# Gated recurrence: score blocks of four tokens as one product around a middle reference, five levels above instead of seven

## The reference

```python
qf = silu(q) * DK ** -0.5
z  = clip(f, -30, 30)
logf = minimum(log_sigmoid(z) + log1p(lb * exp(-z)), 0)      # g, one per token and channel
kf = -expm1(logf)                                            # 1 - decay
# inside a chunk, bcum = cumsum(g):
attn[i, j] = sum_d qf[i, d] * exp(bcum[i, d] - bcum[j, d]) * kf[j, d]     for j <= i
o = attn @ v + (qf * exp(bcum)) @ state
state = exp(b_last) * state + (kf * exp(b_last - bcum)).T @ v
```

## Time and profile before

| | us |
|---|---|
| median of 3 runs | 2405.66 (2405.41 to 2405.76) |
| span of the profiled execution | 2404.5 |
| TensorE busy | 2388.6 (99%) |
| VectorE busy | 1676.1 (70%) |
| GpSimd busy | 1253.3 (52%) |
| ScalarE busy | 811.7 (34%) |
| the heads, from the first head's diagonal to the last head's keys | about 619.6 to 1049.2 |

### The profile page before, as it was taken

One profiled execution on the slowest core, in us unless ns is written; L12 is line 12 of the kernel. 1 busy time (PEld: TensorE's weight loads), 2 busy tenths in 40 slices (PEclk: granted clock), 3 DMA queues, 4 the chain that ended last, 5 costly groups with the idle time before them and its releaser, 6 DMA issues.

```text
span 2404.5 us, 31465 instructions
## 1 busy us (share of the span) xinstructions
PE 2388.6 (99%) x11815; PEld 1967.3 (82%) x11815; DVE 1676.1 (70%) x1837; ACT 811.7 (34%) x1187; POOL 1253.3 (52%) x936
## 2 busy tenths in 40 slices
PE   9999999999999999999999999999999999999998
PEld 6888888888888888888888888888887888888887
DVE  7889888888878888878865637652896534444464
ACT  4443442554222222221122214253444434342422
POOL 0677773343022332223767766745667656666564
PEclk9999999999999999999999999999999999999999
DMA  7322323111211111124854445522532212121243
GB/s 284 140 80 105 127 110 123 62 61 61 78 44 44 44 44 44 44 97 144 277 199 149 140 140 167 181 91 71 177 129 75 92 62 97 59 99 57 84 175 123
DMA packets 93193, 263.28 MB, mean 109 GB/s; under 512 B 8736, under 2 KB 14112, under 8 KB 92064
## 3 DMA queue, kind: packets, MB, share of 16 engines
q1 hardware_dynamic: 77536, 227.26, 27.3%
q10 hardware_dynamic: 15552, 34.61, 4.1%
...
## 4 chain that ended last, share of the span: by engine, by line
PE 94%; DVE 3%; issue 1%; ACT 1%; DMA 0%; SPq 0%; POOL 0%; ACTq 0%; DVEq 0%
PE ps L537 25%; PE ps L538 25%; PE ps L539 25%; PE xb L537 2%; PE xb L538 2%; PE xb L539 2%; PE xa L537 2%; PE xa L539 2%; PE xa L538 2%; PE ps L630 1%; PE xb L771 1%; PE xb L800 1%; PE xb L803 1%; PE xa L791 1%; DVE mt_lo L1138 0%
## 5 line engine op out<-in xcount | busy, mean ns | idle before, releaser
L2822 POOL TENSOR_TENSOR small<-small 128x1 f32<-128x1 f32 x172 | 53.6, 311 | 794.8 <-PE ps L539 620.9
L2825 POOL TENSOR_TENSOR w_lo<-w_raw,w_hi 128x1024 fp32r<-128x1024 f32 x172 | 444.5, 2584 | 14.4
L537 PE MATMUL ps<-h_hi,w_hi 128*128 128x512 f32 x928 | 368.0, 397 | 0.0
L539 PE MATMUL ps<-h_hi,w_lo 128*128 128x512 f32 x928 | 362.0, 390 | 0.0
L538 PE MATMUL ps<-h_lo,w_hi 128*128 128x512 f32 x928 | 361.7, 390 | 0.0
L2911 POOL TENSOR_TENSOR m_lo<-m_raw,m_hi 128x512 fp32r<-128x512 f32 x144 | 200.3, 1405 | 146.1 <-ACT m_hi L2203 142.8
L537 PE MATMUL ps<-yb_hi,w_hi 128*128 128x512 f32 x608 | 238.7, 393 | 0.0
L539 PE MATMUL ps<-yb_hi,w_lo 128*128 128x512 f32 x608 | 236.6, 389 | 0.0
L538 PE MATMUL ps<-yb_lo,w_hi 128*128 128x512 f32 x608 | 236.6, 389 | 0.0
L537 PEld LDWEIGHTS ps<-h_hi,w_hi 128*128 128x128 f32 x928 | 174.3, 188 | 36.9 <-issue 0.2
L539 PEld LDWEIGHTS ps<-h_hi,w_lo 128*128 128x128 f32 x928 | 174.2, 188 | 37.0
...
## 6 DMA issues: line engine op xcount, KB each, us to landing
...
```

The costliest lines, as they stand in the source:

```text
L537: nc.tensor.matmul(out, wh, xh, start=start, stop=False, skip_group_check=onto)
L539: return nc.tensor.matmul(out, wl, xh, start=False, stop=stop, skip_group_check=onto)
L2822: nc.gpsimd.tensor_tensor(small[:, 13:14], small[:, 12:13], small[:, 12:13], ALU.add)
L2825: nc.gpsimd.tensor_tensor(w_lo[:, u], w_raw[:, u], w_hi[:, u].bitcast(F32), ALU.subtract).then_inc(w_split, 1)
```

## The change

The bottom two levels and the diagonal go; blocks of four tokens are scored directly, as one product. In a block of four the reference time is in the middle: the earliest token's key is multiplied by a decay, its query by the inverse of one, the middle token's key and query are copied, and the two latest tokens' queries are multiplied by decays and their keys by inverses. The inverses 1/f are made as the square of Abs_reciprocal_sqrt on ScalarE (`decay_inverses`: three ACTIVATE of 256 elements, a Square and a Copy with scale -1, each of 768), corrected on VectorE by one Newton step (`base_keys`). The decays are kept above 9e-14 (`LEAST`). The products of these keys and queries (`base_blocks`, again 16) replace the diagonal, and their scores enter `attn` through a mask (`base_out`). Five levels, of blocks of 4 to 64, follow. `kr`, `qpf`, `vt` and `zc` serve as scratch, so ScalarE's copy of `vt` now waits until the base keys and queries are ready (`lv_ready`). TensorE runs the whole of tile `i` before `base_blocks`, then waits for tile `g` at once. Levels 1 and 2 stand where levels 3 and 4 stood, 3 and 4 where 5 and 6 stood, 5 where 7 stood.

```diff
@@ -33,7 +33,8 @@
 KEPT = KB // 2
 CHUNK = 128
 NCH = T // CHUNK
-LEVELS = 7
+BASE = 4
+LEVELS = 5
 TIME_ORDER = (0, 1, 2, 3, 7, 6, 5, 4)
 CW, LW = 31, 4
 FFB = 4
@@ -41,6 +42,7 @@
 KV_RING = 6
 EPS = 1e-6
 CLIP = 30.0
+LEAST = 9e-14
 LRU_C = 8.0
 DK_SCALE = float(P) ** -0.5
 XA_HEADS = 4
...
@@ -511,6 +513,7 @@
         down_loaded = [*kvw_loaded, *s_loaded[1], lg_loaded]
         DOWN_OLD = [first + 32 for first in KV_FIRST[:4]] + [16 * (SEVENS // 2)] * 2 + [16 * KB // 2]
         y_gained, GAINED_OLD = mem_rt, 1
+        inv_ready, inv_done, INV_OLD = lm_ready, lmult_done, KB
         HEAD_PAIR = N_HG // 2 + 1 - M0 - SEVENS
         SUM_OLD, BLOCK_OLD, PART_OLD, UP_OLD = 4 * SEVENS, 7 * SEVENS, 3 * SEVENS, 16 * (SEVENS - SEVENS // 2)
@@ -522,6 +525,12 @@
 
             x = x[:]
             return bass.AP(x.tensor, x.offset + at0, [x.ap[0], [step, 2], [skip, n], [one, c]])
+
+        INV = HALF + HALF // 2
+
+        def inv_early(x):
+
+            return pairs(x, HALF, HALF // BASE, HALF // BASE, 1, 1)
 
         def turned(x, n):
@@ -754,7 +763,7 @@
 
             def level(h, l):
 
-                pe.wait_ge(lv_ready, LEVELS * h + l)
+                pe.wait_ge(lv_ready, (LEVELS + 1) * h + l + 1)
                 pe.wait_ge(lv_free, (LEVELS + 1) * h + max(l - 1, 1))
                 w = CHUNK // 2
                 bank = xb[:, (l % 2) * HALF:(l % 2 + 1) * HALF]
@@ -771,11 +780,11 @@
                         mm = nc.tensor.matmul(out_, keys, queries, start=True, stop=True, tile_position=(0, side * w))
                 mm.then_inc(lv_done, 1)
 
-            def diagonal_blocks(c, ch):
+            def base_blocks(c, ch):
                 w = CHUNK // 2
                 for side in range(2):
                     cols = slice(c * CHUNK + side * w, c * CHUNK + (side + 1) * w)
-                    mm = nc.tensor.matmul(xb[side * w:(side + 1) * w, cols], hg["k"][:, cols], hg["q"][:, cols],
+                    mm = nc.tensor.matmul(xb[side * w:(side + 1) * w, cols], hg["kr"][:, cols], hg["qpf"][:, cols],
                                           start=True, stop=True, tile_position=(0, side * w))
                 return mm
@@ -839,26 +848,17 @@
                     full_tile(m, 1)
                 else:
                     tiles_beside_tail(m, h)
-                take(m + 1, 0)
-                half_of(0, 0)
-                if first(h):
-                    quarter_of(0, 1, 0)
-                pe.wait_ge(evac[1], m + 1)
+                full_tile(m + 1, 0)
+                pe.wait_ge(lv_ready, (LEVELS + 1) * h + 1)
                 if not first(h):
                     pe.wait_ge(oc_done, h)
-                per_chunk(NCH, diagonal_blocks).then_inc(diag_done, 1)
-                if first(h):
-                    quarter_of(0, 1, 1).then_inc(mm_done, 1)
-                else:
-                    half_of(0, 1).then_inc(mm_done, 1)
-                level(h, 1)
-                level(h, 2)
+                per_chunk(NCH, base_blocks).then_inc(base_done, 1)
                 take(m + 1, 1)
                 quarter_of(1, 0, 0)
                 quarter_of(1, 0, 1)
                 quarter_of(1, 1, 0)
-                level(h, 3)
-                level(h, 4)
+                level(h, 1)
+                level(h, 2)
                 quarter_of(1, 1, 1).then_inc(mm_done, 1)
                 pe.wait_ge(evac[0], m + 2)
                 if not first(h):
@@ -1518,32 +1518,78 @@
 
             zc, sp_, sn, f, b, k, q, gg = (hg[x] for x in ("zc", "sp", "sn", "f", "b", "k", "q", "gg"))
 
+            def earliest(x):
+
+                return pairs(x, 0, HALF + BASE - 1, HALF // BASE, BASE, 1)
+
+            def middle(x):
+
+                return pairs(x, 1, HALF + 1, HALF // BASE, BASE, 1)
+
+            def latest(x):
+
+                return right(x, BASE // 2)
+
             def queries(h, l, last):
 
-                c = 2 ** (l - 1)
+                c = BASE * 2 ** (l - 1)
                 s.wait(last)
-                if l > 1:
-                    mul(merged(hkp[l % 3], c), left(k, c), left(b, c))
+                mul(merged(hkp[l % 3], c), left(k, c), left(b, c))
                 mul(packed(hqp[l % 4], c), right(q, c), right(f, c)).then_inc(lv_ready, 1)
 
+            def spread(c):
+
+                done(mul(left(b, c), left(b, c), right_end(f, c)))
+                return s.at(mul(right(f, c), right(f, c), left_end(f, c)))
+
             def widen(h, l):
 
-                c = 2 ** (l - 1)
-                dve.wait_ge(lv_ready, LEVELS * h + l)
-                if l == 1:
-                    done(v.tensor_copy(left(b, c), right(f, c)))
-                else:
-                    done(mul(left(b, c), left(b, c), right_end(f, c)))
-                return s.at(mul(right(f, c), right(f, c), left_end(f, c)))
+                dve.wait_ge(lv_ready, (LEVELS + 1) * h + l + 1)
+                return spread(BASE * 2 ** (l - 1))
+
+            def first_decays(h, last):
+
+                s.wait(last)
+                done(v.tensor_copy(left(b, 1), right(f, 1)))
+                mul(right(f, 1), right(f, 1), left_end(f, 1)).then_inc(inv_ready, 1)
+
+            def base_keys(h):
+
+                dve.wait_ge(inv_ready, INV_OLD + h + 1)
+                dve.wait_ge(inv_done, INV_OLD + h + 1)
+                inv, first_, minus = zc[:, 0:INV], hg["qpf"], hg["vt"]
+                mul(packed(zc, 2), latest(f), packed(first_, 2))
+                done(mul(inv_early(zc), earliest(b), inv_early(first_)))
+                done(v.scalar_tensor_tensor(minus[:, 0:INV], inv, -2.0, minus[:, 0:INV], ALU.add, ALU.mult))
+                mul(earliest(hg["kr"]), earliest(k), earliest(b))
+                v.tensor_copy(middle(hg["kr"]), middle(k))
+                mul(latest(hg["kr"]), latest(k), packed(minus, 2))
+
+            def base_queries(h):
+
+                mul(earliest(hg["qpf"]), earliest(q), inv_early(hg["vt"]))
+                v.tensor_copy(middle(hg["qpf"]), middle(q))
+                mul(latest(hg["qpf"]), latest(q), latest(f)).then_inc(lv_ready, 1)
+
+            def base_out(h):
+
+                dve.wait_ge(base_done, h + 1)
+                w = CHUNK // 2
+                v.memset(small[:, 14:15], 0.0)
+                for side in range(2):
+                    part = slice(side * w, (side + 1) * w)
+                    out_, scores = (x[part, :].rearrange("p (n c) -> p n c", c=CHUNK)[:, :, part] for x in (hg["attn"], xb))
+                    ins = v.copy_predicated(out_, lvmask[part, 0].rearrange("p (n c) -> p n c", c=w), scores)
+                ins.then_inc(lv_free, 1)
 
             def scores_out(h, l):
 
-                c = 2 ** (l - 1)
+                c = BASE * 2 ** (l - 1)
                 dve.wait_ge(lv_done, LEVELS * h + l)
                 dve.wait_ge(lv_free, (LEVELS + 1) * h + l)
                 v.memset(small[:, 14:15], 0.0)
                 bank = xb[:, (l % 2) * HALF:(l % 2 + 1) * HALF]
-                v.copy_predicated(right(hg["attn"], c), packed(lvmask[:, l - 1], c), packed(bank, c)).then_inc(lv_free, 1)
+                v.copy_predicated(right(hg["attn"], c), packed(lvmask[:, l], c), packed(bank, c)).then_inc(lv_free, 1)
 
             def states(h):
@@ -1602,49 +1648,41 @@
                     cleared = s.at(v.memset(hg["attn"][:], 0.0))
                 dve.wait_ge(hsig, 2 * h + 2)
                 done(v.scalar_tensor_tensor(f[:], sn[:], lb, sp_[:], ALU.mult, ALU.add))
-                s.at(v.tensor_scalar(f[:], f[:], 1.0, None, ALU.min))
+                s.at(v.tensor_scalar(f[:], f[:], 1.0, LEAST, ALU.min, ALU.max))
                 s.at(v.tensor_scalar(k[:], sn[:], lb1, 0.0, ALU.mult, ALU.max))
-                s.at(v.tensor_scalar(merged(hkp[1], 1), left(sn, 1), lb1, 0.0, ALU.mult, ALU.max))
-                last = s.at(v.memset(right(b, 1), 1.0))
+                first_decays(h, s.at(v.memset(right(b, 1), 1.0)))
                 if not first(h):
                     squares_low(h)
                     gated = gated_output(h, m)
+                base_keys(h)
                 dve.wait_ge(hsigq, h + 1)
                 for n in range(2):
                     ins = v.scalar_tensor_tensor(q[:, n * HALF:(n + 1) * HALF], turned(ps[1], n), DK_SCALE, turned(hg["qs"], n),
                                                  ALU.mult, ALU.mult)
                 ins.then_inc(evac[1], 1)
                 dve.wait_ge(evac[1], m + 1)
-                queries(h, 1, last)
-                last = widen(h, 1)
-                dve.wait_ge(ylru_stored, 16 * KB // 2)
-                queries(h, 2, last)
+                base_queries(h)
                 if not first(h):
                     normed_output(h, gated)
-
-                dve.wait_ge(diag_done, h + 1)
+                dve.wait_ge(ylru_stored, 16 * KB // 2)
+                dve.wait_ge(lv_ready, (LEVELS + 1) * h + 1)
+                queries(h, 1, spread(BASE // 2))
                 if first(h):
                     s.wait(cleared)
```

(40 more changed lines are left out.)

8 lines of the change are left out of this document (4 added, 4 removed).

## The result

| | before | after |
|---|---|---|
| median, us | 2405.70 (2405.41 to 2405.76, 4 runs) | 2422.22 (2421.75 to 2422.26, 4 runs) |
| ratio to before | | 1.0068, 95% interval 1.0054 to 1.0083 |
| span of the profiled execution | 2404.5 | 2420.4 |

The change makes the kernel 16.5 us slower. The forecast was 2408.4 with a range up to 2416: wrong in size, and outside the range. The profiled execution took 2422.19, so what lies around the span is 1.8 us. The forecast had 1.2 for it, from a span and a median of different executions.

A forecast was written before the change was run, and what follows sets the result against it. TensorE, busy 99%, bounds the kernel, with VectorE close behind at kr. Head 0 +5.3 and heads 1 to 6 -2.6 give +2.7 on the span of 2404.5, 2407.2; plus 1.2 to the median: 2408.4 us, range 2401 to 2416 (own range 2404 to 2413).

The forecast's parts named there:

- TensorE's saving: Each head on TensorE: one group of 32 records gone, 1.3 us a head, 10.4 us for 8 heads if nothing waits.
- The new wait for `kr`: Loop heads, TensorE's transposes of kr: 0.9 us new wait a head, keeping 0.4 of 1.3; bounds none to 2.9.
- VectorE becomes the bound at `kr`: Rival, chance 0.25: VectorE's longer chain makes each loop head longer; 2414.5, up to 2422 with short products at 512's length.
- The margin of 0.45: At kr before the change: VectorE is about 0.45 us ahead of TensorE; a larger TensorE gain alone becomes a wait.
- the two `w_lo` meetings: Loop heads: two VectorE products meet GpSimd's running w_lo and wait for its end, 2.07 us each.
- the 1.5 of `base_out`: VectorE's masked base_out, each head: 1.5 us like the multiplication it replaces; up to 2.4 if short runs cost more.
- The larger loss in the last head: Last head: VectorE loses more to GpSimd (2.88 at 1039.90); cited for the VectorE-bound rival, that head's saving counted as nothing.
- first wait: Head 0, TensorE before the base blocks: wants them at 622.3, VectorE ready at 624.6, so a wait of 2.3 us.
- The second wait of 4.3: Head 0, TensorE before tile g: waits 4.3 us for the low part VectorE makes behind base_out, ready at 630.0.
- The clock: Rival, chance 0.10: head 0's idle of 4.3 us halves TensorE's clock; +2.7 or +8.2 us, so 2411 to 2416.6.
- The table loads: ScalarE: two more loads at 1.28 us each, not the skill page's 2.66; by the page head 0 is 1.4 longer.
- The weights' transfer: Next head's load comes 2.8 us later; w_lo ends at 751.1, needed at 751.5, so it just fits.

The follow-up runs named there:

- experiment 4: Changed kernel with GpSimd's weight splits left out of the heads' loop (it only signals; weight parts stale): 2405.74 us, 0.9998 to the kernel before.
- experiment 5: Changed kernel with one of GpSimd's four high parts of a loop head not made, its low part made from a stale one: 2417.49 us, ratio 1.0049.
- experiment 3: Changed kernel with the base blocks' short operands on VectorE and ScalarE in contiguous runs instead of every fourth element: 2417.05 us, ratio 1.0048.
- experiment 6: Kernel before the change without TensorE's products of levels 1 and 2, all VectorE work kept: 2405.38 us, ratio 0.9999.
- 1: Changed kernel; in head 0 VectorE makes tile g's low part right behind base_queries instead of behind base_out: 2418.41 us, ratio 1.0053.
- 2: Changed kernel with 15 extra TensorE products into a free bank behind head 0's base blocks, filling its second wait: 2421.98 us, ratio 1.0068.
- 10: Changed kernel; head 0 does q before inverses and base_keys, then tile g's low part, and 12 products of tile g before the base blocks: 2412.42 us, ratio 1.0027.
- 11: Changed kernel with TensorE's tail of a head later, head 0 with q first, and qpf written behind the clipping of zc: 2397.99 us, ratio 0.9968.
- 12: Kernel before the change, with only TensorE's later tail of a head and the moved qpf: 2406.78 us, ratio 1.0003.
- experiment 8: Changed kernel; head 0 makes tile g's high part before the inverses, its low part while waiting, 12 tile g products before the base blocks: 2415.84 us, ratio 1.004.
- 9: Changed kernel with head 0's tile g weights and 12 products earlier, plus TensorE's levels 3 to 5, kr transposes and chunk states later: 2405.23 us, ratio 0.9999.

## Why the prediction was wrong

The sum gave a span of 2407.2, and it was 2420.4. Of the 13.2 us between them 10.0 are the loop's (7.4 longer instead of 2.6 shorter) and 3.2 head 0's (8.5 instead of 5.3).

- **TensorE's saving: right.** A group of 1.3 is gone from each head (round 55.88 in experiment 4), 256 records fewer.
- **The new wait for `kr`: the step that failed.** "New wait: 0.9 us a head" measured 2.3, in two places. The waits were in the rival *VectorE becomes the bound at `kr`*, which named this mechanism and a price up to 2422; I had given it 0.25. That its top of 2422 is the measured time is luck: it counted 5.3 for head 0 and 1.6 for a loop head, with a masked copy of 2.4 that is not there; measured were 8.5 and 1.1. Two sizes of the chain were off. The meeting with `w_hi` was not counted at all: 0.7 us a head (experiment 5). The products and copies on lone elements had been priced by length alone: 0.66 a head (experiment 3, 58.30 to 57.64). Together they are the 1.4 that were missing; no run takes out both at once. The margin of 0.45, the two `w_lo` meetings, the first product held until 0.55 behind `w_lo`, and the 1.5 of `base_out` (against the bound of 2.4) came as written.
- **What I should have asked.** I moved the low parts along with TensorE and the transfer, and never asked where the high part of 1.5 us ahead of each would land; I counted meetings of the kind that the earlier trace rows show and no other. The high part does not always start free of VectorE: experiment 6 shows it landing on a product as soon as TensorE's release comes earlier, and the changed kernel shows it where the transfer's release comes later. The larger loss in the last head stood there as a sign, and I gave it to the rival. The 0.90 at 753.93 in the earlier trace rows, which I booked as friction, ends 0.54 behind the high part of 752.79. And the product just ahead of that of the earlier trace rows is held by a high part for 0.9, which the prediction does not count. VectorE and GpSimd, before:

```profile
1038.41 1.56 DVE L1153 TENSOR_TENSOR hg_kp<-hg_k,hg_b 128x512 f32<-128x512 f32 x1
```

```profile
1038.40 1.04 POOL L2823 TENSOR_SCALAR w_hi<-w_raw 128x1024 fp32r<-128x1024 f32 x1
```

- **Head 0: mechanism right, first wait too small.** 3.5 instead of 2.3. The lone elements account for 1.0 of the 1.2 (the wait is 2.5 in experiment 3). The second wait of 4.3 and its releaser were as forecast.
- **The clock: the rival came true, for another reason.** I tied it to the wait of 4.3; experiments 1 and 2 show that the 3.5 ahead of it suffices. Its price was 1.5 us, below the rival's 2.7, because more than half of the slow stretch (628.0 to 634.9) was spent waiting, until 631.7.
- **The table loads: right, for the loop.** In head 0 the load back lasted 1.28 and the sigmoid started 0.01 behind it, as in the trace before. The Trainium skill's drain of 1.38 (ScalarE: Activation LUTs, "What ACT_TABLE_LOAD costs") did not appear as time on ScalarE here either:

```profile
619.60 1.28 ACT L2467 ACT_TABLE_LOAD   x1
620.89 1.03 ACT L2467 ACTIVATE hg_qs<-ps 128x1024 f32<-128x1024 f32 x1
```

- **The weights' transfer: right.** No wait of TensorE for a weight appears in the loop.

Shown by runs of their own: that the loop's loss goes when all collisions go (4), the high part's share (5), the spacing's share (3), head 0's share (10), the first wait as enough for the clock's fall (1, 2), and that the saving arrives once TensorE asks later (11, 12). Open: why the clock fell in experiment 8 and not in 9, and what filling the second wait is worth (2).
